# The causal mask as a matrix product, and turned rows moved into and around two attentions

## The reference, cut to what matters

```python
z = einsum('gts,bcsgd->bctgd', tril(w_s), v) + b_s      # mixing, y_a = gelu(u) * z * silu(g)
s = einsum('bhmqd,bhmkd->bhmqk', q, k) * scale          # differential attention, q and k of width 32
s = where(kpos[None, :] <= qpos[:, None], s, -inf)      # the causal mask
pd = softmax(s)[:, :, 0] - lam * softmax(s)[:, :, 1]
x = x + concatenate([y_a, y_b, y_m]) @ w_out
```

## Time and profile before

| | us |
|---|---|
| median of 3 runs | 916.38 (915.25 to 921.18) |
| the profiled execution | 915.04 |
| its span, first to last instruction | 913.3 |
| TensorE busy in it | 875.5 |
| VectorE, ScalarE, GpSimd busy | 611.5, 410.9, 111.4 |

### The profile page before, as it was taken

How to read it: one execution, slowest core, us unless ns; L and a number is a source line. 1 busy time by engine, 2 the same in 40 slices (tenths; PEclk the granted TensorE clock), 3 DMA queues, 4 the chain that set the end, 5 groups by cost and what they waited for, 6 DMA issues and landing times.

```text
span 913.3 us, 16032 instructions
## 1 busy us (share of the span) xinstructions
PE 875.5 (96%) x6422; PEld 820.9 (90%) x6422; DVE 611.5 (67%) x1155; ACT 410.9 (45%) x727; POOL 111.4 (12%) x123
## 2 busy tenths in 40 slices
PE   6999999899999999989999999999999999999996
PEld 6998998898888777888999999999998999999994
DVE  4784687662979789745686478945665776676672
ACT  6456666231011254735344875444344444453451
POOL 0149666100011000400000000100000000000000
PEclk9999999999999899999999999999999999999998
DMA  9454433281452400344665243654453455645741
GB/s 368 169 183 126 123 104 111 79 334 49 140 174 103 184 1 1 93 152 142 215 217 168 94 135 110 220 184 175 149 188 134 141 181 187 229 142 182 231 139 47
DMA packets 37786, 139.41 MB, mean 153 GB/s; under 512 B 4304, under 2 KB 4432, under 8 KB 37456
## 3 DMA queue, kind: packets, MB, share of 16 engines
q1 hardware_dynamic: 37424, 136.90, 43.8%
q10 hardware_dynamic: 288, 1.48, 0.5%
HBM read 137.32 MB, written 1.05 MB: 152 GB/s over the span
## 4 chain that ended last, share of the span: by engine, by line
PE 88%; DVE 7%; issue 2%; ACT 2%; DMA 1%; POOL 0%; DVEq 0%; SPq 0%; ACTq 0%; POOLq 0%
PE psum L578 21%; PE psum L579 21%; PE psum L580 21%; PE psum L577 15%; PE psum L731 3%; PE psum L713 2%; PE psum L652 1%; PE psum L724 1%; DVE h_rows L1748 1%; PE psum L856 1%; DVE w_lo L1594 1%; DVE h_lo L1560 1%; DMA rows<-in_mem 1%; PE psum L641 1%; ACT act_tmp L1219 0%
## 5 line engine op out<-in xcount | busy, mean ns | idle before, releaser
L1594 DVE TENSOR_TENSOR w_lo<-raw,w_hi 128x1024 fp32r<-128x1024 f32 x180 | 212.2, 1222 | 86.2 <-ACT w_hi L1151 85.1
L1151 ACT ACTIVATE w_hi<-raw 128x1024 fp32r<-128x1024 f32 x204 | 206.0, 1052 | 41.3 <-PE psum L580 30.3
L578 PE MATMUL psum<-h_hi,w_hi 128*128 128x256 f32 x704 | 199.5, 283 | 0.6 <-issue 0.6
L579 PE MATMUL psum<-h_lo,w_hi 128*128 128x256 f32 x704 | 199.2, 283 | 0.0
L580 PE MATMUL psum<-h_hi,w_lo 128*128 128x256 f32 x704 | 199.2, 283 | 0.0
L578 PE MATMUL psum<-w_hi,h_hi 128*128 128x256 f32 x576 | 166.6, 289 | 4.1 <-DVE h_lo L1560 4.1
L580 PE MATMUL psum<-w_hi,h_lo 128*128 128x256 f32 x576 | 163.7, 284 | 0.0
L579 PE MATMUL psum<-w_lo,h_hi 128*128 128x256 f32 x576 | 163.6, 284 | 0.0
L578 PEld LDWEIGHTS psum<-h_hi,w_hi 128*128 128x128 f32 x704 | 135.1, 192 | 1.6 <-issue 1.4
L579 PEld LDWEIGHTS psum<-h_lo,w_hi 128*128 128x128 f32 x704 | 135.1, 192 | 0.2
L580 PEld LDWEIGHTS psum<-h_hi,w_lo 128*128 128x128 f32 x704 | 135.1, 192 | 0.0
(11 more groups left out here) (276 smaller groups left out, 1138.5 us busy)
## 6 DMA issues: line engine op xcount, KB each, us to landing
raw<-in_blocks SPq DMA_DIRECT2D x208, 512.0 KB, 4.4
first<-in_blocks SPq DMA_DIRECT2D x40, 512.0 KB, 4.8
w_late<-in_blocks SPq DMA_DIRECT2D x4, 512.0 KB, 7.6
early<-in_early SPq DMA_DIRECT2D x1, 1579.0 KB, 16.3
attention<-in_late ACTq DMA_DIRECT2D x1, 1376.0 KB, 6.9
rows<-in_mem SPq DMA_DIRECT2D x2, 512.0 KB, 4.3
x<-in_x SPq DMA_DIRECT2D x1, 1024.0 KB, 8.4
out_x<-h_rows SPq DMA_DIRECT2D x2, 512.0 KB, 2.6
```

Source lines behind the costliest of these rows:

```text
L578: nc.tensor.matmul(out, lhs[0], rhs[0], start=start, stop=False, skip_group_check=shared_bank)
L579: nc.tensor.matmul(out, lhs[0], rhs[1], start=False, stop=False, skip_group_check=shared_bank)
L1151: nc.scalar.activation(split_part(w_hi, q), raw[:, q % RAW_SLOTS, :], ACT.Copy).then_inc(w_hi_ready, 1)
L1594: V.tensor_tensor(split_part(w_lo, q), raw[:, q % RAW_SLOTS, :], split_part(w_hi, q).bitcast(F32), ALU.subtract).then_inc(w_lo_vector, 1)
```

## The change

The mask becomes a matmul. ACT writes two float32r tiles once, the identity and the block of the causal constant (`mask_parts`); `pair_scores` then adds identity times block onto each diagonal block right behind that block's scores, over all 128 rows of the array; the addition on DVE is gone. z, ym0 (layer 0) and ym1 (layer 1) move into the units, at steps 16, 17, 14 and 20, with their gating and copies. Two filler steps are issued ahead of each layer's first scores. In `out_project` the last rows are turned ahead of the first two column quarters, and the wait for their copies stands behind these. x1 is turned inside the second half of `kv1`. The low part of `("out0", 1)` moves out of the `y_b1` norm to behind it, and layer 1's y_d product ahead of ya1's copies.

```diff
+FILL_AHEAD = 2
+TURN0_AT = {14: "ym0", 16: "z0", 17: "z1"}
+YM1_AT = 20
-LOW_BESIDE_NORM = {"q": both_of(["m_qg0"]), "k": both_of(["b_v"]), "y_b1": [("out0", 1)]}
+LOW_BESIDE_NORM = {"q": both_of(["m_qg0"]), "k": both_of(["b_v"])}
...
+        mask_parts = sb("mask_parts", [P, 2, P], F32R)
...
# TensorE
+                turn_others()
                 for c in range(n_early):
                     begin((f"out{layer}", c))
                     add(c, early_k)
-                turn_others()
+                turned(pe, *names)
                 for c in range(n_early):
                     add(c, late_k)
...
                         mm = nc.tensor.matmul(psum[:, SCORE_BANK + score.slot(i + j), u.seg(t)],
-                                              q[:, t * P:(t + 1) * P], k[:, 0:u.keys[t]], start=True, stop=True)
+                                              q[:, t * P:(t + 1) * P], k[:, 0:u.keys[t]], start=True, stop=True,
+                                              skip_group_check=u.causal)
+                        if u.causal:
+                            at = u.seg(t).start + t * P
+                            mm = nc.tensor.matmul(psum[:, SCORE_BANK + score.slot(i + j), at:at + P], mask_parts[:, 0, :],
+                                                  mask_parts[:, 1, :], start=False, stop=True, skip_group_check=True)
...
+            filler0 = (s for name, half in FILL[0] for s in rows_piece(name, half, h_t))
+            for _ in range(FILL_AHEAD):
+                next(filler0)
             turned(pe, "k0", "k1", "mq0")
             turned(pe, "q0", "q1", "mk0")
+            pe.wait_ge(mask_ready, 1)
...
-                n, issued = len(units), 0
+                n, issued = len(units), FILL_AHEAD
...
+            def turns0(i):
+                name = TURN0_AT.get(i)
+                if name == "ym0":
+                    normed.wait(pe, "y_m0")
+                    turn_pair("ym0", lambda a, t: rows[:, t, 3840 + a * P:3840 + (a + 1) * P])
+                elif name is not None:
...
+            for _ in rows_piece("kv1", 0, mem_t):
+                pass
+            for n, _ in enumerate(rows_piece("kv1", 1, mem_t)):
+                if n == 3:
+                    normed.wait(pe, "x1")
+                    for j in range(3):
+                        turn_x1(j)
+                elif n == 6:
+                    turn_x1(3)
             turned(pe, "x1_2", "x1_3")
...
+                if i == YM1_AT:
+                    normed.wait(pe, "y_m1")
+                    turn_pair("ym1", lambda a, t: rows[:, t, 1792 + a * P:1792 + (a + 1) * P])
# ScalarE
+            link(nc.scalar.activation(mask_parts[:, 0, :], ident, ACT.Copy))
+            nc.scalar.activation(mask_parts[:, 1, :], E("causal")[:, 0:P], ACT.Copy).then_inc(mask_ready, 1)
# VectorE
-                elif u.causal:
-                    corners = [v.rearrange("p (b k) -> p b k", k=P)[:, 0:3:2, :] for v in (bank[:, 0:3 * P], E("causal"))]
-                    link(V.tensor_tensor(corners[0], corners[0], corners[1], ALU.add))
...
+                if i == 12:
+                    normed.mark(V.tensor_tensor(rows[:, :, 3840:4096], rows[:, :, 3584:3840], rows[:, :, 3840:4096],
+                                                ALU.mult), "y_m0", vec)
+                elif TURN0_AT.get(i - 2) == "ym0":
+                    source_lo("ym0", ym_t, 0, 0.5)
+                elif name in ("z0", "z1"):
+                    gate_values(int(name[1]))
+                    if name == "z1":
+                        normed.mark(V.memset(lam_tmp[:, 7:8], 0.0), "y_a0", vec)
...
+            yb = heads(rows, 1536 + HC, 4, 64)
+            for step in range(2):
+                norm_step(step, "y_b1", yb, E("b_subln"))
             for j in range(2):
                 source_lo(f"ya0_{j}", h_t, 2 * j, 0.25)
-            link(grouped_norm("y_b1", heads(rows, 1536 + HC, 4, 64), E("b_subln")))
+            norm_step(2, "y_b1", yb, E("b_subln"))
+            link(norm_step(3, "y_b1", yb, E("b_subln")))
             normed.mark(gate_yb(1), "y_b", vec)
-
+            split_to(OUT[0] + 3)
```

More of the change, by code:

```diff
@@ L262, in xpose_names @@
     out += ["mk0", "q0", "q1", "k0", "k1", "mq0"]
-    out += [("unit", i) for i in range(len(UNITS0))]
-    out += ["z0", "z1", "ym0", "ya0_0", "ya0_1", "yb0_0", "yb0_1"]
+    for i in range(len(UNITS0)):
+        out += [TURN0_AT[i]] if i in TURN0_AT else []
+        out += [("unit", i)]
+    out += ["ya0_0", "ya0_1", "yb0_0", "yb0_1"]
     out += [f"x1_{j}" for j in range(4)] + ["mk1", "cmp", "dq0", "dq1", "dk0", "dk1", "hid_k", "hid_v", "mq1", "hid_t", "kvc", "kc"]
@@ L673, in out_rest, with out_project @@
                 ends(half, rest_done, layer + 1)
[L675 removed]
+            def out_project(layer, early_k, turn_others, names, n_early):
                 late_k = [k for k in range(KT) if k not in early_k]
@@ L781, in operands0, with layer_units @@
                         lambda kb: rows[:, kb, 2560 + 64 * u.head:2624 + 64 * u.head])
-            def layer_units(layer, units, base, operands, filler, ahead=lambda i: None):
-                n, issued = len(units), 0
+            def layer_units(layer, units, base, operands, filler, ahead):
+                n, issued = len(units), FILL_AHEAD
                 pair_scores(base, units[0:2], operands)
@@ L798, in layer_units @@
                     pass
[L801 to L812, removed]
+            def turns0(i):
[4 more added lines that the diff above has]
+                elif name is not None:
+                    t = int(name[1])
+                    pe.wait_ge(ws_ready, 1)
+                    normed.wait(pe, "a_v")
+                    xpose.claim(pe, name)
+                    for g in range(4):
+                        mm = nc.tensor.matmul(psum[:, XPOSE_BANK + xpose.slot(name), g * P:(g + 1) * P],
+                                              ws_masked[:, g * P:(g + 1) * P], rows[:, t, 512 + g * P:512 + (g + 1) * P],
+                                              start=True, stop=True)
+                    fill(xpose, mm, name)
+            layer_units(0, UNITS0, 0, operands0, filler0, turns0)
             normed.wait(pe, "y_a0")
@@ L822, in turn_last, with turn_x1 @@
                     turn_pair(names[j], lambda a, t: rows[:, t, c0 + (2 * j + a) * P:c0 + (2 * j + a + 1) * P])
[L823 to L829, removed]
-                turn_pair(f"x1_{j}", lambda a, t: h_rows[:, t, (2 * j + a) * P:(2 * j + a + 1) * P])
+            out_project(0, range(0, 4), lambda: turn_last(3072, "y_b", ("yb0_0", "yb0_1")), ("yb0_0", "yb0_1"), 2)
+            def turn_x1(j):
+                turn_pair(f"x1_{j}", lambda a, t: h_rows[:, t, (2 * j + a) * P:(2 * j + a + 1) * P])
+            for _ in rows_piece("kv1", 0, mem_t):
[7 more added lines that the diff above has]
+                    turn_x1(3)
             turned(pe, "x1_2", "x1_3")
@@ L892, in _ @@
             fill(xpose, mm, "kc")
+            filler1 = (s for name, half in FILL[1] for s in rows_piece(name, half, h_whole))
+            for _ in range(FILL_AHEAD):
+                next(filler1)
             turned(pe, "dq0", "dq1", "mk1", "dk0", "dk1", "kc", "mq1")
@@ L923, in _ @@
                 turn_pair(f"ya1_{j}", lambda a, t: rows[:, t, 3584 + (2 * j + a) * P:3584 + (2 * j + a + 1) * P])
-            normed.wait(pe, "y_m1")
-            turn_pair("ym1", lambda a, t: rows[:, t, 1792 + a * P:1792 + (a + 1) * P])
             out_rest(1)
             turned(pe, "ya1_0", "ya1_1")
-            out_project(1, range(0, 4), lambda: turn_last(2560, "y_d", ("yb1_0", "yb1_1")), 2)
+            out_project(1, range(0, 4), lambda: turn_last(2560, "y_d", ("yb1_0", "yb1_1")), ("yb1_0", "yb1_1"), 2)
             keep_clock(xpose, XPOSE_BANK, "x2_0", 8)
@@ L1348, in _ @@
             square_sums("x1", x)
-            for half in range(2):
-                memory_rows(1, half)
+            memory_rows(1, 0)
             even_sources("x1_", h_whole[0], E("l1_norm"))
+            memory_rows(1, 1)
             for half in range(2):
@@ L1376, in gate_conv @@
             def gate_conv(i):
+                if i == YM1_AT + 1:
+                    source_hi("ym1", ym_t[0], 0.5)
                 if i in (20, 22):
@@ L1918, in gate_yb, with gate_values @@
                                        rows[:, :, 1536 + HC * part:1536 + HC * (part + 1)], ALU.mult)
-            def extra0(i):
+            def gate_values(t):
+                arrive(xpose, f"z{t}")
+                for g in range(4):
+                    c = slice(g * P, (g + 1) * P)
+                    ins = V.scalar_tensor_tensor(rows[:, t, c], psum[:, XPOSE_BANK + xpose.slot(f"z{t}"), c],
+                                                 E("a_bs")[:, g:g + 1], rows[:, t, c], ALU.add, ALU.mult)
+                xpose.freed(ins, f"z{t}", vec)
+            def extra0(i):
+                name = TURN0_AT.get(i - 1)
+                if i == 12:
[7 more added lines that the diff above has]
```

(3 more changed lines are left out.)

26 lines of the change are left out of this document (14 added, 12 removed).

## The result

The changed kernel takes 953.66 us (median of 4 runs, 946.74 to 955.68) against 918.72 beside it: a ratio of 1.037, 95% interval 1.030 to 1.044. The forecast was 934, range 914 to 946: the sign was right, and the 19.0 us forecast are little more than half of the 34.9 between the medians. The profiled execution's span is 953.9, 40.6 over the 913.3 of before; it is the longest of its four, that of before is shorter than all of its own, so the traces show a larger loss than the medians.

A forecast was written before the change was run, and what follows sets the result against it. TensorE, busy 96% of the span, was taken as the bound. Mask +16.2 and +14.3, less 0.7, 5.3, 1.5 and 4.0, gave +19.0 on 915.0: 934 us, range 914 to 946.

The forecast's parts named there:

- last unit product to `out_rest`: Behind layer 0's units: the waits for y_m0 and y_a0, 1.07 and 1.89 us, go.
- `out_rest` to `kv1`: Layer 0's output: the 2.08 us copy wait goes, 1.5 credited for the clock, less a new y_b wait of 1.2.
- `kv1` to the next product: Turning x1: waits of 0.57 and 1.09 us go into `kv1`'s second half, about 0.2 left: -1.5.
- layer 1's end: Behind layer 1's units: waits of 0.34, 1.69 (ym1's copies) and 1.99 us (yb1's copies) go: -4.0.
- The mask at full clock: Causal pairs in both layers' units: masks on TensorE add 2.03 us a pair, +16.2 in layer 0, +14.3 in layer 1.
- Its switches: Array changes between all rows and some: 8 instead of 2 a pair, 0.19 us each, 1.14 us a pair.
- its masks: Streaming four masks of 128 float32r columns a pair: 0.06 us each, 0.24 us together.
- its last rival: Dearer masks: float32r at 128 columns as slow as float32, 10.2 us more, 944 us; chance 0.06.
- The first rival: Array does not empty for a mask, weights load while scores stream: 0.24 us a pair, 905 us; chance 0.11.
- The moves: All rearrangements besides the mask: -0.7 fillers, -5.3 behind layer 0's units, -1.5 at x1, -4.0 at layer 1's end.
- Work moved into the units: z, ym0 and ym1 cost TensorE what they did; filler covers their PSUM bank waits, so nothing taken.
- the two fillers: Steps ahead of first scores: layer 0 -0.7 us (0 to -1.42); layer 1 0 (-1.6 to +1.9).

The follow-up runs named there:

- moves alone: The changed kernel without the mask's two tiles and matmuls, the mask addition back on VectorE; 904.73 us, ratio 0.9862 against the kernel before.

## Why the prediction failed

Stage by stage, between the starts of TensorE's instructions in the profiled executions:

| us | before | after | moves alone | forecast change | measured |
|---|---|---|---|---|---|
| layer 0's units | 78.13 | 107.96 | 78.89 | +16.2 (mask) | +29.07 over the moves alone |
| last unit product to `out_rest` | 6.71 | 1.50 | | -2.96, and z and ym0 leave | -5.21 |
| `out_rest` to `kv1` | 33.55 | 30.92 | | -2.4 | -2.63 |
| `kv1` to the next product | 17.60 | 15.96 | | -1.5 | -1.64 |
| from there to layer 1's first scores | 95.74 | 97.85 | | 0 | +2.11 |
| layer 1's units | 76.31 | 99.65 | 76.49 | +14.3 (mask) | +23.16 over the moves alone |
| layer 1's end | 35.83 | 30.71 | | -4.0, and ym1 leaves | -5.12 |

**The mask at full clock: right.** 2.11 us a pair against 2.03. Its switches were priced a little too high (0.19 for 0.17), its masks too low by half (0.06 for 0.11). At full clock layer 0's units would come to some 78.89 + 8 x 2.11 = 95.8 us; 94 were forecast, 107.96 measured.

**The clock: the step that failed.** The forecast multiplied a pair's price by 16 as if the units ran at 1.00 throughout. It named the lower clock only inside its last rival, as one that "would act alike, 1.5 us for each stretch like the one at 177.90", and gave that 0.06 without counting stretches. Nine stood at masked pairs, of 3.4 or 6.8 us, 44.4 in all, and at half the clock that is 22.2 us withheld. The rows above give the same: 0.13 x 107.96 + 0.10 x 99.65 = 24.0 us in the units; with the moves alone it is nothing in layer 0 and 0.02 x 76.50 = 1.5 in layer 1. The 22.5 between them fill the gap between the forecast's 16.2 + 14.3 = 30.5 and the mask's measured 29.07 + 23.16 = 52.2, which is 21.7. A warning stood in the earlier trace rows: at 308.50 TensorE held 15 instructions in 6.10 us, and the clock was at 0.50.

**The first rival: refuted.** A switch costs 0.17 us, and the masks' weights were not loaded ahead. This agrees with the Trainium skill's "TensorEngine Tiling (Array Packing)", Key Properties, by which a change of tiling mode drains TensorE. The load ahead that the rival took from the skill's "TensorE: Matmul & The Clock Gate", Part 2, first step, does not show at this change: the load at 113.41 begins with its matmul, behind 0.33 of idle time.

**The moves: right as a whole** (12.5 against 11.5), and in the waits that they removed. Work moved into the units cost no wait in layer 0: z and ym0 came in (2.13 us for 16 products and some 0.4 for four transposes behind the units of before), two filler steps (12 products of 0.12, 1.4) went out, and the units grew by 0.76, to 78.89. Layer 1's, with ym1 inside, took 76.49 against 76.31. The whole is nearer than its parts, whose errors cancel in part: layer 1's end gave 5.12, some 0.5 of it ym1's transposes, where 4.0 stood. Off were the two fillers. Layer 0's gave 0.3, from 1.42 of idle to 1.13, because the turn ahead of it now ended at 75.53 and GpSimd's low part came at 76.66. Layer 1's cost 1.2 us by the traces, toward the upper end of the stated -1.6 to +1.9: without them the units start 1.82 earlier (300.74 against 302.56) and take 0.66 more. The steps run at 0.50, the first scores come later, and the next wait, for the exponentials, is 1.98 at 336.49 in the changed kernel.

**What stays open:** why one masked pair brings a fall and the next does not, and why the executions of one kernel differ in this (0.971 to 0.980). Nor do the runs separate the switch as such from the time in which nothing streams because of it, some 8 x 0.17 = 1.4 us of a masked pair by the price above, which the profile counts as busy: no run has the one without the other. For the second speaks that the lower clock without masks stands beside waits, at 308.50 in the earlier trace rows, and in the stretch at 0.91 behind the wait of 2.08 in the earlier trace rows.

## What to carry to other kernels

Group TensorE's work by the rows that it uses: all of a pair's scores, then all of its masks, instead of one behind the other, turned 953.7 us into 908.0 with the same products, one start flag aside. After any change that breaks dense work on TensorE into pieces, read the granted clock of the stretch beside the busy share, and in a forecast price the loop at both levels. On the engine that sets the time even the cheap order costs: 0.45 us a pair, 3.6 in layer 0's units, for work that VectorE did beside.

## What was not expected of the hardware

- TensorE can be busy 100% by the profile and be granted 0.83 to 0.90; each fall among the masked pairs came in or right behind a pair in which it changed between all rows and some rows eight (or six) times.
- Lengthening the same pair to 4.19 us with dense masks, or to 3.93 with scores side by side, left the clock at 1.00 in layer 0's units.
- A 128-column mask product on all rows costs 0.11 us in a row of them, what a transpose of 128 columns costs (three in 0.32).
- Two units' scores in different rows overlap even when the list holds them one unit after the other (3.38 us instead of 3.93).
